# Projections, branches and output weights of two decoder layers as seven quarter-size products, with weight sums on GpSimd

## What is computed

```python
n = rms_norm_2(h, mix_norm_g[l])
proj = jnp.einsum("btd,de->bte", n, w_in[l])
q, k, v, qi, ki, wi, xr, yg, cv, gt = _split_cols(proj)
...                                  # top-k attention, gated recurrence, 31-tap convolution
merged = (g_attn * jnp.einsum("bte,ed->btd", attn, w_o_attn[l])
          + g_rnn * jnp.einsum("bte,ed->btd", rnn, w_o_rnn[l])
          + g_conv * jnp.einsum("bte,ed->btd", cnv, w_o_conv[l]))
h = h + jnp.einsum("btd,de->bte", merged, w_out[l])
...
a = jax.nn.silu(jnp.einsum("btd,df->btf", f, w_ffn_gate[l])) * jnp.einsum("btd,df->btf", f, w_ffn_up[l])
h = h + jnp.einsum("btf,fd->btd", a, w_ffn_down[l])
```

## Time and profile before

| | us |
|---|---|
| median of 3 runs | 1823.98 |
| lowest, highest | 1812.88, 1826.47 |
| the profiled execution | 1818.04 |
| its span on the core | 1816.3 |
| its mean granted clock | 0.989 |
| PE, PEld, DVE, ACT, POOL busy | 1760.9, 1449.7, 953.2, 492.5, 328.5 |

### The profile page before, as it was taken

The page is one execution under the profiler, slowest core; times in us unless marked ns, Lnnn a source line. Parts: engine busy times, 40 slices in busy tenths (PEclk is TensorE's granted clock), DMA queues, the critical chain, the costliest instruction groups (busy, mean ns, idle before and its releaser), DMA issues.

```text
span 1816.3 us, 32164 instructions
## 1 busy us (share of the span) xinstructions
PE 1760.9 (97%) x13454; PEld 1449.7 (80%) x13454; DVE 953.2 (52%) x1907; ACT 492.5 (27%) x1064; POOL 328.5 (18%) x349
## 2 busy tenths in 40 slices
PE   8999998899999999999999999999999999989999
PEld 3344654789877888788888999978888888889999
DVE  0222725566546857566315675348667563157662
ACT  2112236444343123742102100051146422020000
POOL 0000600465100000000003555300000000036553
PEclk9999999899999999999999999999999999999999
DMA  7411310000044333333343444443434334434453
GB/s 313 172 47 70 116 47 1 3 4 5 36 183 157 134 123 139 139 119 113 139 139 125 163 162 164 153 162 126 153 131 147 119 115 158 144 135 168 163 172 108
DMA packets 53360, 225.46 MB, mean 124 GB/s; under 512 B 5088, under 2 KB 29024, under 8 KB 29280
## 3 DMA queue, kind: packets, MB, share of 16 engines
q1 hardware_dynamic: 53216, 223.40, 34.7%
HBM read 222.34 MB, written 1.05 MB: 123 GB/s over the span
## 4 chain that ended last, share of the span: by engine, by line
PE 90%; DVE 4%; ACT 3%; SPq 1%; issue 1%; DVEq 1%; DMA 0%; POOL 0%; ACTq 0%
PE PS L519 26%; PE PS L714 14%; PE PS L660 13%; PE PS L1893 9%; PE PS L738 8%; PE PS L1399 2%; PE PS L1412 2%; PE PS L1832 2%; PE PS L1986 1%; PE PS L532 1%; PE PS L633 1%; SPq L1800 1%; PE PS L602 1%; PE PS L614 1%; PE PS L1907 1%
## 5 line engine op out<-in xcount | busy, mean ns | idle before, releaser
L519 PE MATMUL PS<-arena,ring 128*128 128x272 f32 (+1 forms) x2176 | 498.1, 389 | 0.0
L519 PEld LDWEIGHTS PS<-arena,ring 128*128 128x128 f32 x2176 | 411.2, 190 | 77.2 <-issue 1.4
L660 PE MATMUL PS<-arena,ring 128*128 128x272 f32 (+1 forms) x1024 | 229.5, 386 | 2.1 <-DVE arena L1187 2.1
L979 DVE SCALAR_TENSOR_TENSOR arena<-arena,par 128x272 f32<-128x272 f32 (+1 forms) x480 | 214.8, 488 | 16.7 <-issue 1.3
L660 PEld LDWEIGHTS PS<-arena,ring 128*128 128x128 f32 x1024 | 194.2, 190 | 36.0 <-DVE arena L1187 2.9
L938 POOL TENSOR_TENSOR arena<-ring 128x512 f32<-128x512 f32 (+1 forms) x32 | 40.0, 1251 | 1000.9 <-DMA ring<-stream_dram 1000.7
L714 PE MATMUL PS<-arena 128*128 128x136 f32 (+1 forms) x1280 | 156.1, 281 | 8.4 <-DVE arena L943 8.4
L1893 PE MATMUL PS<-arena,ring 128*128 128x512 f32 (+2 forms) x448 | 158.3, 514 | 1.7 <-DVEq L2192 1.7
L714 PEld LDWEIGHTS PS<-arena 128*128 128x128 f32 x1280 | 152.5, 195 | 8.8 <-issue 8.8
L1893 PEld LDWEIGHTS PS<-arena,ring 128*128 128x128 f32 (+1 forms) x448 | 84.0, 189 | 75.0 <-issue 69.0
L753 ACT ACTIVATE arena<-PS 128x272 f32<-128x272 f32 (+1 forms) x144 | 55.6, 393 | 323.6 <-PE PS L519 313.7
(11 more groups left out here) (352 smaller groups left out, 2337.7 us busy)
## 6 DMA issues: line engine op xcount, KB each, us to landing
ring<-stream_dram SPq DMA_DIRECT2D x185, 1024.0 KB, 4.8
ring<-stream_dram SPq DMA_DIRECT2D x32, 512.0 KB, 3.9
ring<-stream_dram SPq DMA_DIRECT2D x16, 384.0 KB, 3.8
arena<-x_dram SPq DMA_DIRECT2D x1, 2048.0 KB, 11.6
cst<-const_dram SPq DMA_DIRECT2D x1, 1080.0 KB, 7.0
out_dram<-H SPq DMA_DIRECT2D x4, 256.0 KB, 2.9
cst<-const_dram SPq DMA_DIRECT2D x1, 912.0 KB, 17.3
arena<-stream_dram SPq DMA_DIRECT2D x1, 512.0 KB, 7.1
```

The source lines that it names most:

```text
L519: last = mm(PS[:, (m + f) % 4, nw], lslot(l, n, KD, 256)[:, k, P * f:P * f + P], NT[:, k, nw], start=k == 0, stop=k == KD - 1)
L660: last = mm(PS[:, i % 4, NQ], lslot(l, n, KD, 256)[:, k, P * (i % 2):P * (i % 2) + P], src[:, k, NQ], start=k == 0, stop=k == KD - 1)
L979: stt(CVG[:, c, NQ], CVA[:, c, j + Q0:j + T2], dw_w[l][:, c, j:j + 1], CVG[:, c, NQ], ALU.mult, ALU.add)
```

## The change

The fifty slots `j` = 0 to 49 are done in the seven-product form too. The products are named a, b, c, d, e, g, h. a, b and d read weight quarters as they came, e a quarter that has been overwritten in the ring; c, g and h read sums. The token side of c, g, e and d reads differences of halves. The results are not kept apart: a, c, e and d are chained in one PSUM region, each product adding to what stands there, and between them ACT copies out the state after a, after c, after e and after d. g and h share a second region, which b's stands beside. Per slot then: 28 matmuls, five copies by ACT of 136 (128) columns, and two additions by DVE, `sum_f0` (L1395, from PSUM and the copies) and `sum_f1` (L1407, copies alone).

Projections take all 272 tokens in both layers; branches and output weights take `NQ`. PE issues e and d of slot j-1 among the products of slot j. POOL makes all weight sums of the fifty slots (`mix_sums`) into two buffers by turns, and the token halves of two branches; DVE makes the other halves. The order of the slots changes (`LSTREAM`), the gates of the branches share two buffers, attention writes out one group of heads after each round, and `CONV_PLAN` says up to which unit the long convolution has come in each slot. The other functions of ACT now work on two to four tiles at once in place (`open_gates`, `open_branch`).

```diff
-            def project(n, m, nw):
-                lslot_wait(pe, l, n)
-                for f in range(2):
-                    if m + f >= 4:
-                        pe.wait_ge(L["kept"], B["kept"] + m + f - 3)
-                    for k in range(KD):
-                        last = mm(PS[:, (m + f) % 4, nw], lslot(l, n, KD, 256)[:, k, P * f:P * f + P], NT[:, k, nw],
-                                  start=k == 0, stop=k == KD - 1)
-                    last.then_inc(L["made"], 1)
...
+            def product_g(j, ks=range(4)):
+                if ks[0] == 0:
+                    summed(j, 1)
+                    if j >= 2:
+                        pe.wait_ge(L["mixes"], B["mixes"] + f0_at(j - 2))
+                last = product(banks(j)[2], MS[j % 2][:, 0], operands(j)[2][0], start=True, ks=ks)
...
+            def product_c(j):
+                summed(j, 2)
+                pe.wait_ge(L["copies"], B["copies"] + COPIES["a", j])
+                product(banks(j)[0], MS[j % 2][:, 1], operands(j)[2][1]).then_inc(L["products"], 1)
...
+            def before(j):
...
+                if j == OC_J:
+                    pe.wait_ge(L["conv_out"], B["conv_out"] + 1)
+                    pe.wait_ge(L["conv_halves"], B["conv_halves"] + 1)
...
+            for j in range(MIXES):
+                before(j)
+                if j < WO_J:
+                    product_a(j)
...
+                    if j:
+                        product_e(j - 1)
+                    product_g(j)
...
+                product_c(j)
+                if j and j != WO_J:
+                    product_d(j - 1)
+                within(j)
+                product_h(j)
+                product_b(j)
...
+            def sum_f0(j):
...
+                dve.wait_ge(L["copies"], B["copies"] + COPIES["a", j])
+                dve.wait_ge(L["copies"], B["copies"] + COPIES["c", j])
+                dve.wait_ge(L["products"], B["products"] + PRODUCTS["b", j])
+                made = PS[:, 2 * (j % 2) + 1, 0:2 * n].rearrange("p (i t) -> p i t", i=2)
...
+                tt(mix_to(l, j)[0], made, copies(j)[0][:, :, 0:n], ALU.add).then_inc(L["mixes"], 1)
...
+            def mix_sums(j):
+                w11, w12, w21, w22 = quarters(l, mix_slot(j))
+                to = MS[j % 2]
+                lslot_wait(pool, l, mix_slot(j))
+                if j >= 2:
+                    pool.wait_ge(L["products"], B["products"] + PRODUCTS["b", j - 2])
+                g.tensor_tensor(to[:, 0], w21, w22, ALU.add).then_inc(L["summed"], 1)
+                g.drain()
+                g.tensor_tensor(to[:, 1], to[:, 0], w11, ALU.subtract).then_inc(L["summed"], 1)
+                g.drain()
+                g.tensor_tensor(to[:, 2], w12, to[:, 1], ALU.subtract).then_inc(L["summed"], 1)
+                g.tensor_tensor(w21, w11, w21, ALU.subtract).then_inc(L["summed"], 1)
```

More of the change, by code:

```diff
@@ L227, in build @@
         NT = cut(0, KD, T2)
-        AT = cut(0, KD, T2)
         QIb = cut(2176, 4, T2)
@@ L606, in tensor_layers, with product, operands @@
-            pe.wait_ge(L["swap_used"], B["swap_used"] + 3)
+            def product(out, w, tokens, start=False, ks=range(4)):
+                for k in ks:
+                    last = mm(out, w[:, k], tokens[:, k], start=start and k == 0, stop=k == 3, skip_group_check=True)
+                return last
+            def operands(j):
+                src, halves_of = mix_source(j)
+                n0, n1 = mix_halves(l, j)
+                x = src.rearrange("p (k e) t -> p k e t", e=2)
+                n = n0.stop - n0.start
+                return x[:, :, 0], x[:, :, 1], [halves_of[:, i, :, 0:n] for i in range(4)], n0, n1
@@ new lines, in product_d, with logits @@
+            def product_d(j):
+                pe.wait_ge(L["copies"], B["copies"] + COPIES["e", j])
+                product(banks(j)[0], quarters(l, mix_slot(j))[3], operands(j)[2][3]).then_inc(L["products"], 1)
+            def logits(i):
+                t, g = divmod(i, 2)
+                nk = slice(0, KEYS[t + 1])
+                if i == 0:
+                    pe.wait_ge(L["wi_kept"], B["wi_kept"] + 1)
+                    pe.wait_ge(L["iroped"], B["iroped"] + 2)
+                else:
+                    pe.wait_ge(L["relu"], B["relu"] + i)
+                for j in range(4):
+                    h = 4 * g + j
+                    last = mm(PS[:, 4 + j, nk], QIb[halves(h % 2), h // 2, META + P * t:META + P * t + P],
+                              KIb[halves(h % 2), nk], start=True, stop=True)
+                last.then_inc(L["logits"], 1)
@@ new lines, in scalar_layers, with width, copy_a @@
+            a(WT, PS[64:72, 6, NW], ACT.Copy)
+            for h in range(2):
+                last = a(KIb[halves(h), :], PS[0:64, 6, NW], ACT.Copy)
+            last.then_inc(L["kept"], 1)
+            def width(j):
+                n = mix_halves(l, j)[0]
+                return n.stop - n.start
+            def copy_a(j):
+                act.wait_ge(L["products"], B["products"] + PRODUCTS["a", j])
+                if j >= 2:
+                    act.wait_ge(L["mixes"], B["mixes"] + f0_at(j - 2))
+                n = width(j)
+                a(copies(j)[0][:, 0, 0:n], PS[:, 2 * (j % 2), 0:n], ACT.Copy).then_inc(L["copies"], 1)
@@ new lines, in open_branch, with exponents @@
+            def open_branch(to, j, done):
+                act.wait_ge(L["mixes"], B["mixes"] + f1_at(j - 1))
+                nc.scalar.drain()
+                last = a(to, to, ACT.Sigmoid)
+                if done:
+                    last.then_inc(L["gts"], 1)
+            R = rounds(l)
+            def exponents(r):
+                t, _ = R[r]
+                rows, nk = QT[t][1], KEYS[t]
+                act.wait_ge(L["max"], B["max"] + r + 1)
+                for j in range(4):
+                    last = a(SB[0:rows, j, 0:nk], SB[0:rows, j, 0:nk], ACT.Exp, bias=NM[0:rows, j:j + 1],
+                             accum_out=SM[0:rows, j:j + 1])
+                last.then_inc(L["exp"], 1)
@@ new lines, in keep_turned @@
+            def keep_turned(r):
+                t, _ = R[r]
+                rows = QT[t][1]
+                act.wait_ge(L["pt_made"], B["pt_made"] + r + 1)
+                tiles = key_tiles(t)
+                whole = sum(n == P for _, n in tiles)
+                for s in range(whole):
+                    last = a(PT[:, s, :, 0:rows], PS[:, 4:8, P * s:P * s + rows], ACT.Copy)
+                for s in range(whole, len(tiles)):
+                    n = tiles[s][1]
+                    last = a(PT[0:n, s, :, 0:rows], PS[0:n, 4:8, P * s:P * s + rows], ACT.Copy)
+                last.then_inc(L["pt_kept"], 1)
```

932 lines of the change are left out of this document (605 added, 327 removed).

## The result

The changed kernel takes **2064.6 us** (median of four runs, 2057.6 to 2069.3) where the kernel before takes 1820.7 in the same series: a ratio of 1.134, 95% interval 1.128 to 1.140. The prediction was 1936, range 1850 to 1990: the direction and the mechanism came true, the size did not. The profiled span is 2063.9 us against 1816.3, 248 us more, where 118 were forecast.

A forecast was written before the change was run, and what follows sets the result against it. DVE, held by POOL's weight sums, was taken to bound slots 8 to 41. Layer 0 summed 50 + 336 + 12 + 66 = 464 us (+56), layer 1 454 (+62); 1818 + 118 = 1936 us, range 1850 to 1990.

The forecast's parts named there:

- PE's slot: Fifty slots a layer: 56 records each, 6.42 us for 7.33 in layer 0; 79.5 us saved were PE the bound.
- What DVE gets: DVE's own work in layer 0: 268 us, of which 217 in slots 8 to 41.
- The price of a meeting: Slots 8 to 41: each POOL operation costs DVE 0.96 us, 131 us a layer, less 12 for operations not held.
- What the meetings cost the middle: Slots 8 to 41 of layer 0: DVE's stretch grows from 217 to 336 us, beyond PE's 251.
- rival A: PE stays the bound because DVE's lag doesn't reach it: 1779 us, chance 0.10.
- The base without meetings: Slots 8 to 41 of layer 0 with PE as bound: 251 us of PE work plus 12.
- the end of the convolution: Layer norm chain before slot 42: ACT's serial pieces make both PE and DVE stand, about 12 us a layer.
- The ends: Slots 1 to 7 take 50 us, slots 42 to 50 take 66 (64 in layer 1), no meeting loss added.
- rival D: POOL itself ends last in slots 1 to 7 and 42 to 50: 13 us more, inside the range, no own chance.
- B: Half the loss, 0.5 us a POOL operation, since POOL often runs while DVE waits: 1811 us, chance 0.07.
- C: PE's clock falls as well behind its waits in 68 slots: 66 us more, 2002 us, chance 0.10.
- DVE near 100%: Profile sign: windows in slots 8 to 41 with DVE near 100% busy and PE near 70%.

The follow-up runs named there:

- run 13: Changed kernel without weight sums and 30 of 31 convolution taps, gates two slots later, convolution's end three slots earlier: 1798.6 us, 0.988 of the kernel before.
- run 1: Changed kernel with POOL's four weight sums a slot shrunk from 512 columns to 2, all waits and signals kept: 1858.9 us, 1.022 of the kernel before.
- run 7: Kernel before plus four unneeded two-input POOL operations of 488 columns in each of 34 slots a layer: 1927.8 us, ratio 1.059.
- run 2: Changed kernel, each of POOL's four operations a slot reading one 512-column tile times 1 instead of adding two: 1898.6 us, 1.044 of the kernel before.
- run 9: Changed kernel without weight sums and without 30 of the long convolution's 31 taps: 1841.7 us, 1.010 of the kernel before.
- run 6: Changed kernel with all sums, gates two slots later and the convolution's end three slots earlier: 2022.0 us, 1.110 of the kernel before.
- run 10: Changed kernel with all weight sums by POOL but 30 of the long convolution's 31 taps left out: 1904.5 us, 1.044 of the kernel before.
- run 5: Changed kernel without weight sums, gates two slots later and the convolution's end three slots earlier: 1844.8 us, 1.013 of the kernel before.

## Why the prediction missed, step by step

Layer 0 took 115 us more where 56 were forecast. I go by the steps.

**PE's slot: right; its work beside the slots was put too low.** In undisturbed slots the intervals are 6.5 us (the last three of layer 0 in the changed kernel are), against 6.42 forecast. The middle as a whole had 251 us of PE's work; PE is busy 259 in run 13 at a clock of 0.99.

**What DVE gets: right.** In run 1 DVE is busy 216.4 us in the middle; the prediction had 217.

**The price of a meeting: right in kind, a tenth high.** The term was 131 less 12 us in slots 8 to 41, 119; DVE's busy time gives 108 (0.80 a POOL operation, 0.70 in run 7). The Trainium skill ("SBUF — State Buffer", section "Who interferes with whom") states an exclusive lock between a DVE instruction with two SBUF inputs and a GpSimd instruction that reads SBUF. With both operations of two inputs the traces agree; with one input on POOL's side run 2 shows 0.22 us instead of 0.80.

**What the meetings cost the middle: right to the microsecond, partly by luck.** The sum held 348 us with meetings (336 + 12) and, as rival A, 263 without (251 + 12): 85 between them. Measured: 380.3 and 295.1, 85.2 between them. The luck: the 85.2 hold things that the sum had not, the slower clock (0.87 for 0.95) and 12 us that stay with one-input operations (307.4 in run 2). The level was wrong, not the difference.

**The base without meetings: the step that failed first.** The sum had 251 us of PE's work and 12 us for "the end of the convolution", 263. Run 1's middle takes 295.1: PE is busy 262.0 of them, 11 more, and idle 33.1, 21 more. Its waits around slots 41 and 42, where the convolution ends:
```profile
PE PS L609 <- DVE arena L1276: 19.7, 2, 15.2
PE PS L643 <- issue: 8.5, 1, 8.5
```
The second is no wait for "issue": PE goes on when DVE's last token half is done (`before` of slot 43; in the changed kernel at 1015.75, the half ends at 1015.65). So the term of 12 us measured 28. Run 13 is the test of it: with the end moved under products, PE's idle time in the middle falls from 23 us (run 9) to 8.

At the gates, priced at nothing, PE waits 2.9 us in run 1, but 7.2 in the changed kernel, and DVE 10.5. PE waits for ACT; ACT stands in order behind `swap_halves` (L1002), which waits for DVE's rotation; and DVE then waits for ACT. The changed kernel, PE, ACT and DVE in turn:
```profile
695.76 7.58 PE L761 MATMUL PS<-arena,ring 128*128 128x272 f32 x24 [7.23 <-ACT arena L1141]
```
```profile
691.68 1.11 ACT L1002 ACTIVATE arena<-arena 64x1088 f32<-64x1088 f32 x1 [7.01 <-DVE arena L1473]
```
```profile
705.62 0.30 DVE L1413 TENSOR_TENSOR arena<-arena 128x136 f32<-128x136 f32 x1 [10.50 <-ACT arena L1045]
```
At the end of the convolution I had summed ACT's own pieces, and left out that each step of the chain crosses engines while all of them stand still. DVE there, in the changed kernel:
```profile
988.17 2.42 DVE L1548 SCALAR_TENSOR_TENSOR arena<-PS,arena 128x2176 f32<-128x2176 f32 x1 [1.43 <-PE PS L609]
991.97 0.44 DVE L1405 TENSOR_TENSOR arena<-PS,arena 128x272 f32<-128x272 f32 x1 [1.37 <-PE PS L643]
994.72 0.30 DVE L1413 TENSOR_TENSOR arena<-arena 128x136 f32<-128x136 f32 x1 [2.31 <-ACT arena L1045]
997.49 0.72 DVE L1525 TENSOR_TENSOR arena<-arena 128x544 f32<-128x544 f32 x1 [2.47 <-ACT arena L1058]
...
1005.19 2.43 DVE L1542 TENSOR_TENSOR arena<-arena 128x2176 f32<-128x2176 f32 x1 [3.66 <-ACT arena L976]
1011.83 1.58 DVE L1293 TENSOR_TENSOR arena<-arena 128x544 f32<-128x544 f32 x1 [4.21 <-ACT arena L1244]
```
Six waits, 15 us, on the one engine that I had called the bound; all but the third are as long in run 1, within 0.1 us, so they are the chain's own. PE waits in the same stretch 21.3, 4.5 and 9.3 us. In the whole middle DVE is idle 56 us, where the sum gave it 12; the two moves of run 6 took 18 us off the stretch. So 32 of the 59 us that layer 0 is over the forecast lie in the base: 295 measured for 263. That the base is the same in the changed kernel is inferred, from the difference of 85 that came out as forecast.

**The ends: the step that failed second.** I had put the meetings in slots 1 to 7 and 42 to 50 at nothing, since DVE has time there. But PE waits there for single DVE and POOL operations, and one that is held is late however idle its engine is on average. At the start PE waits 3.8 us for POOL's second token halves and 5.7 for ACT's first copy (none and 3.7 in run 1). Near the end of the stage it waits 6.3 for DVE's merged halves; the same wait in the changed kernel, in run 1 and in run 2:
```profile
PE PS L643 <- DVE arena L1298: 6.3, 1, 6.3
```
```profile
PE PS L643 <- DVE arena L1298: 0.8, 1, 0.8
```
```profile
PE PS L643 <- DVE arena L1298: 1.2, 1, 1.2
```
The difference of the changed kernel and run 1 at the ends is 9 + 4 + 7 = 20 us in layer 0; run 10 against run 9, with DVE idle half of the middle, gives 21. Run 2 is only 2 us above run 1 at the ends, with POOL's operations at full length, so it is the meeting there too and not POOL's own work. Layer 1 goes the same way: 373.0 for 287.9 in the middle, 65.0 for 58.1 at the end. The prediction's rival D had named the place, with 13 us for both layers.

**The account.** Layer 0: 32 (base of the middle) + 20 (meetings at the ends) = 52 of 59 us over the forecast. The other 7, and the 16 us outside the changed slots, are not explained by any run. Layer 1 is 55 us over its forecast (117 for 62); its middle took 373.0 us for 328 + 12 = 340, 33 of them.

**The rivals.** B is out. A, as an alternative, is out, but its time was also my base, and it was 80 us too low: 1779 against 1858.9 in run 1. C: its sign, a granted clock under 0.9 over the stage, did come: 0.87 and 0.88 in the two middles (0.95 in run 1's of layer 0), and PE is busy 25 us longer there for the same records. How much of that lies on the path was not separated, so its price stays open. It is no cause beside the meetings, since the clock was back at 0.95 when only POOL's sums were taken away; it may be a way by which they cost.

**What I had said the profile would show.** Convolution steps over 0.8 us: 0.826. PE waiting for DVE 2 to 3 us in each slot: five waits in 34 slots for a slot's first sum, 25.6 us. One PE pause of some 15 us at slot 42: three, of 21.3, 4.5 and 9.3. POOL 300 us a layer and more: 291. PE near 70% in the middle: 75%. DVE near 100%: 85%, and this is the row that gives the miss away: an engine that is the bound for 325 us and still idle for 55 has waits of its own, and those were priced at 12. Product records at 115 ns: 140 of busy time each over the whole kernel, 131 in run 1; how much of it is the clock was not separated.

## What to carry to other kernels

GpSimd is no free engine beside a VectorE that reads two operands from SBUF: each two-input operation of 488 to 512 columns of the one cost the other 0.7 to 0.8 us here, whoever waits for the result, and at places where TensorE waits for a single sum it costs even when VectorE has time. Before a change is priced by the saved streaming, its own base needs a price: walk through the new order once for every place where three engines hand on one result, and count the crossings, not only the work. A long interval is no wait until the busy time inside it is taken off: the gates looked like 12 us of loss before run 5, and PE waits 2.9 there. And when a run without the suspected cost is no faster than before, the change itself is what doesn't pay: here an eighth of the streaming of fifty slots was worth 80 us on paper; PE's busy time fell by 54 at best (1706.5 us in run 13 for 1760.9), by 36 in run 1, and waits took more than that.

## What the runs showed of the hardware that I had not expected

- GpSimd (POOL) operations with one SBUF input of 512 columns hold DVE's two-input operations little (589 ns a step against 504 undisturbed), those with two inputs much (829), although the one-input operations last longer (1.57 us against 1.33).
- 272 POOL operations whose results nobody reads make a kernel 6% slower in which TensorE is busy 97% of the span: 953 us of DVE work become 1143.
- Taking 30 of 31 convolution taps off DVE changed the kernel before by nothing (0.9995, 0.997 to 1.002), and the one without sums by 17 us.
- A DVE operation need not be long or have two inputs to be held. In the changed kernel the `TENSOR_SCALAR` of 8 columns at the head of a layer (L1333, one input in SBUF) takes 1.24 us on average of the two layers, beside a POOL sum; in run 1 it takes 0.17. Layer 0:
```profile
548.57 1.25 DVE L1333 TENSOR_SCALAR smalls<-smalls 128x8 f32<-128x8 f32 x1
```
